# A whole-model kernel on one core: weight layouts packed into single transfers, a chunk fetched in quarters, PSUM copies put on one engine, and a third of the modulation sums placed elsewhere

## The reference, cut to what matters

```python
# adaptive modulation: six vectors of D per layer (shift, scale, gate for the mixer, then for the experts)
mod = silu(c) @ ada_w[l] + ada_b[l]                       # ada_w: (2, 1024, 6*1024)
h   = rms_norm(x, norm_mix[l]) * (1 + scale) + shift
def mix_gla_gdn(h, w_in, ...):                            # layer 0
    qa, ka, va, ga, za, qkvb, ab, bb, zb = _split(h @ w_in, AB_SPLITS)   # 512x1024 times 1024x3608
    gk = log_sigmoid(ga @ gla_w2 + gla_b) / 16
    oa = rms_norm(gla_chunked(qa, ka, va, gk)) * silu(za)
    qkvb = silu(causal_depthwise_conv(qkvb, conv_w))
    ob = rms_norm(gated_delta_chunked(...)) * silu(zb)
    return concatenate([oa, ob]) @ w_out
def moe(h, ...):  # every token takes 2 of 16 experts
    y = y + combine[:, e:e+1] * (silu(t @ w_gate[e]) * (t @ w_up[e]) @ w_down[e])
```

## Time and profile before

| | |
|---|---|
| median of 3 runs | 1425.98 us |
| time of the profiled execution | 1426.02 us |
| its span, first to last instruction | 1424.2 us |
| PE busy | 1232.5 us (87%) |
| DVE busy | 1066.1 us (75%) |
| ACT busy | 700.7 us (49%) |
| POOL busy | 327.7 us (23%) |
| mean granted clock of PE | 0.927 |
| moved by DMA | 337.68 MB |

### The profile page before, as it was taken

How to read it: one execution, slowest core, us unless ns; L and a number is a source line. 1 busy time by engine, 2 the same in 40 slices (tenths; PEclk the granted TensorE clock), 3 DMA queues, 4 the chain that set the end, 5 groups by cost and what they waited for, 6 DMA issues and landing times. The chain is left out here.

```text
span 1424.2 us, 16421 instructions
## 1 busy us (share of the span) xinstructions
PE 1232.5 (87%) x6452; PEld 931.3 (65%) x6452; DVE 1066.1 (75%) x1278; ACT 700.7 (49%) x918; POOL 327.7 (23%) x129
## 2 busy tenths in 40 slices
PE   2788996867999689999999859967995999999992
PEld 2567885657844668888888634434455788888881
DVE  6666885676845659989999657867266699999994
ACT  4222443232522247777777432248221577777770
POOL 0100000010000005466654200000001145566541
PEclk9899998989999589999999969979995999999996
DMA  9989435026031669999999092462016699999944
GB/s 363 284 292 315 133 119 192 15 94 263 2 123 46 261 211 376 383 381 369 380 373 378 25 366 76 135 233 105 16 64 231 242 368 380 370 385 388 379 176 193
DMA packets 60820, 337.68 MB, mean 237 GB/s; under 512 B 11885, under 2 KB 12638, under 8 KB 45636
## 3 DMA queue, kind: packets, MB, share of 16 engines
q1 hardware_dynamic: 48948, 313.11, 59.0%
q0 software_dynamic: 11360, 22.38, 4.5%
q10 hardware_dynamic: 432, 1.10, 0.2%
HBM read 325.08 MB, written 28.84 MB: 249 GB/s over the span
## 5 line engine op out<-in xcount | busy, mean ns | idle before, releaser
L1433 PE MATMUL ps<-ring_r,work_r 128*128 128x512 f32 x536 | 213.6, 399 | 0.0
L2476 DVE TENSOR_TENSOR ring_r<-ring,early_mod_r 128x2048 fp32r<-128x2048 f32 x76 | 182.4, 2429 | 25.7 <-ACT early_mod_r L1593 25.2
L1593 ACT ACTIVATE work<-ps 128x512 f32<-128x512 f32 (+3 forms) x125 | 84.3, 681 | 235.4 <-PE ps L1433 136.7
L849 POOL TENSOR_TENSOR work<-work,early_mod 128x1024 f32<-128x1024 f32 x30 | 162.5, 5416 | 147.2 <-ACT work L1593 147.2
L1431 PE MATMUL ps<-early_mod_r,work_r 128*128 128x512 f32 x468 | 188.9, 404 | 7.7 <-DVE work_r L2779 4.7
L1432 PE MATMUL ps<-early_mod_r,work_r 128*128 128x512 f32 x468 | 185.0, 395 | 0.0
L1593 ACT ACTIVATE work_r<-ring 128x2048 fp32r<-128x2048 f32 (+2 forms) x87 | 133.7, 1558 | 85.6 <-PE ps L954 85.4
L1593 ACT ACTIVATE early_mod_r<-ring 128x2048 fp32r<-128x2048 f32 x79 | 147.5, 1909 | 0.3 <-PE ps L1433 0.3
L1431 PE MATMUL ps<-work_r 128*128 128x512 f32 x324 | 132.6, 409 | 6.8 <-DVE work_r L2779 4.7
L2476 DVE TENSOR_TENSOR ring_r<-ring,work_r 128x2048 fp32r<-128x2048 f32 x52 | 130.7, 2538 | 4.5 <-ACT work_r L1593 4.5
L1432 PE MATMUL ps<-work_r 128*128 128x512 f32 x324 | 129.5, 400 | 0.0
(11 more groups left out here) (320 smaller groups left out, 2311.0 us busy)
## 6 DMA issues: line engine op xcount, KB each, us to landing
ring<-in_moe_w_up_dram SPq DMA_DIRECT2D x33, 2048.0 KB, 10.4
early_mod<-in_ada_w_dram SPq DMA_DIRECT2D x80, 512.0 KB, 4.5
ring<-in_moe_w_gate_dram SPq DMA_DIRECT2D x19, 2048.0 KB, 9.6
hT<-in_moe_w_down_dram SPq DMA_DIRECT2D x16, 2048.0 KB, 9.9
ring<-in_moe_w_down_dram SPq DMA_DIRECT2D x15, 2048.0 KB, 10.2
work<-in_moe_w_gate_dram SPq DMA_DIRECT2D x14, 2048.0 KB, 10.5
ring<-in_ab_w_in_dram SPq DMA_DIRECT2D x7, 2048.0 KB, 10.1
ring<-in_ada_w_dram SPq DMA_DIRECT2D x8, 1024.0 KB, 17.1
```

Of the source, the lines that this page charges most:

```text
L849: return nc.gpsimd.tensor_tensor(yb[buf], yb[buf], mod[:, 5 * D:6 * D], ALU.mult)
L1433: return mm(out, a_hi, w_lo, start=False, stop=last_)
L1593: return nc.scalar.activation(out, in_, fn, **kw)
L2476: v.tensor_tensor(half_of(l, m, half, True), half_of(l, m, half), highs[(2 * m + half) % MHIGHS].bitcast(F32), ALU.subtract).then_inc(SV.s ...
```

## The change

It has six parts.

1. The 24 columns of chunk 1 are packed on the host to one array of 128 rows by 192 values (`ab_small`) and fetched by one transfer; the 12 parameters in SBUF's `par` area come as one array `params` by one transfer, so that POOL issues 2 parameter loads in place of 13.
2. Chunks 4 to 7 are fetched in quarters of 512 KB: `load_ab_quarter(n + 3, q)` stands in step (n, q) of SP's queue for n = 1 to 4, ahead of that step's side loads. Before, the whole chunk n + 4 stood behind step n's side loads.
3. All copies out of PSUM in the projection are ACT's, but that of `small`, which is DVE's.
4. Odd chunks use banks 4 and 7 in place of 0 and 1 for tiles 0 and 1 (`job_bank`); PE waits for the last copy of the same bank (`last_in`).
5. 5 sides in place of 6 stand in the projection, and 3 in place of 2 in the mixers: `mix_sides` takes 8, 2, 4, 2 and four times 2 steps. In chunk 0 stand 2 steps in place of 8, in chunks 4 to 6 four each in place of 5, in chunk 7 six in place of 5, in chunks 2 and 3 ten each as before. In step q = 3 DVE takes its side steps between and behind its copies.
6. In the overflow block `split_low(j, 2, 1)` moves ahead of `hidden_`.

```diff
--- before.py
+++ after.py
@@ -384,7 +386,8 @@
 
         def loaded(c):
 
-            return 16 * (c // RING + 1)
+            last_ab = first[("abo", 0)] - 1
+            return 16 * (c // RING + 1 + (3 if c > last_ab - RING else 0))
 
         def slot(c):
             return ring[:, c % RING]
@@ -473,8 +476,8 @@
         smallT = carve("work", SEQ)
 
         SIDE = [(0, 2 + i) for i in range(4)] + [(1, i) for i in range(6)]
-        SIDE_A = 6
-        per_step = {0: (2, 2, 2, 2), 1: (0, 0, 0, 0), 2: (2, 3, 2, 3), 3: (2, 3, 2, 3), 4: (1, 1, 1, 2), 5: (1, 1, 1, 2), 6: (1, 1, 1, 2), 7: (2, 2, 1, 0)}
+        SIDE_A = 5
+        per_step = {0: (0, 0, 0, 2), 1: (0, 0, 0, 0), 2: (2, 3, 2, 3), 3: (2, 3, 2, 3), 4: (1, 1, 1, 1), 5: (1, 1, 1, 1), 6: (1, 1, 1, 1), 7: (3, 2, 1, 0)}
         side_at, _u = [], 0
         for n in range(8):
             for c in per_step[n]:
@@ -616,12 +619,17 @@
 
         split_chunks = [(first[("ab", 0)] + n, 24 if n == 1 else 512, 3 * 2048) for n in range(8)]
 
+        def small_weights(of, c):
+            return of[:, c % RING].rearrange("p k f -> p (k f)")[:, 0:KD * SMALL].rearrange("p (k f) -> p k f", k=KD)
+
         def quarter(i):
 
             c, w, at_ = split_chunks[i // 4]
             k = slice(2 * (i % 4), 2 * (i % 4) + 2)
             high = area_r["work"][:, at_ + D * (i % 3):at_ + D * (i % 3) + D].rearrange("p (k f) -> p k f", k=2)
-            return ring[:, c % RING, k, 0:w], high[:, :, 0:w], area_r["ring"][:, c % RING, k, 0:w]
+            if w == SMALL:
+                return small_weights(ring, c)[:, k], high[:, :, 0:w], small_weights(area_r["ring"], c)[:, k]
+            return ring[:, c % RING, k], high, area_r["ring"][:, c % RING, k]
 
         def quarter_used(i):
 
@@ -646,7 +654,7 @@
             if kind == "small" and t:
                 emptied.append(emptied[-1])
                 continue
-            e = "s" if kind in ("za", "zb") or j % 2 else "v"
+            e = "v" if kind == "small" else "s"
             emptied.append((e, counts[e]))
             counts[e] += 1
 
@@ -660,6 +668,10 @@
             emptied.append((e, counts[e]))
             counts[e] += 1
         NJ = len(jobs)
+
+        def job_bank(n, t):
+            return bank((4, 7, 2, 3)[t] if n % 2 else t)
+
 
         def emptier(j):
 
@@ -706,12 +718,13 @@
             def load_ab(n):
                 c = first[("ab", 0)] + n
                 if n == 1:
-                    free(c)
-                    sp.dma_start(slot(c)[:, :, 0:RANK], rows(a["ab_w_in"][0], slice(C_GA, C_GA + RANK))
-                                 ).then_inc(small_in, 16)
-                    load(c, slot(c)[:, :, RANK:RANK + 8], rows(a["ab_w_in"][0], slice(C_AB, C_AB + 8)))
+                    load(c, small_weights(ring, c), a["ab_small"].rearrange("p (k f) -> p k f", k=KD))
                 else:
                     load(c, slot(c), rows(a["ab_w_in"][0], slice(AB_COLS[n], AB_COLS[n] + 512)))
+
+            def load_ab_quarter(n, q):
+                c, k = first[("ab", 0)] + n, slice(2 * q, 2 * q + 2)
+                load(c, slot(c)[:, k], rows(a["ab_w_in"][0], slice(AB_COLS[n], AB_COLS[n] + 512))[:, k])
 
             def side_load(u):
                 i, k = u // KD, u % KD
@@ -745,11 +758,11 @@
                 side_load(u)
             for n in range(8):
                 for q in range(4):
+                    if 1 <= n < 5:
+                        load_ab_quarter(n + 3, q)
                     for u in side_at[4 * n + q]:
                         if u + 3 < KD * SIDE_A:
                             side_load(u + 3)
-                if n + 4 < 8:
-                    load_ab(n + 4)
             side_put(SIDE_A - 1)
             for u in range(KD * SIDE_A, KD * SIDE_A + 3):
                 side_load(u)
@@ -910,19 +923,8 @@
 
             nc.gpsimd.memset(side_pad, 0.0).then_inc(pad_ready, 1)
             pool.wait_ge(chunk_in[0], 32)
-            param(w2aug[0:SMALL + 1, :], a["gate_rows"])
-            param(conv_w.rearrange("p c k -> p (c k)"), a["conv_cols"])
-            param(gla_gain, bc(a["gla_norm"][0]))
-            param(gdn_gain, bc(a["gdn_norm"][0]))
-            param(q_gain, bc(a["swa_q_norm"][0]))
-            param(k_gain, bc(a["swa_k_norm"][0]))
-            param(sink, bc(a["swa_sinks"][0]))
-            param(router_w, a["router_w"].rearrange("(p k) e -> p k e", p=P))
-            param(router_b, bc(a["router_bias"]))
-            param(a_log, bc(a["gdn_a_log"][0]))
-            param(dt_bias, bc(a["gdn_dt_bias"][0]))
+            param(params, a["params"])
             param(pos_i[:], a["pos_cols"])
-            param(gain_col, a["gain_cols"])
             pool.wait_ge(phase_done, 3 * 2)
             for z_ in (xt, vn, st_b[:, 0], ku_b):
                 nc.gpsimd.memset(z_, 0.0).then_inc(init_pool, 1)
@@ -1012,22 +1015,24 @@
                         _, high, low = quarter(qi)
                         for t in ((0, ) if kind == "small" else range(TT)):
                             j = 4 * n + t
-                            if q == 0 and n:
-                                pe.wait_ge(*emptier(j - 4))
-                            if q == 0 and n == 2 and t:
-                                pe.wait_ge(*emptier(j - 8))
                             if n == 0 and t == 0:
                                 pe.wait_ge(norm_act.sem, norm_act.at(0, f"hi{2 * q + 1}"))
                                 pe.wait_ge(norm_dve.sem, norm_dve.at(0, f"lo{2 * q + 1}"))
+                            place = (n % 2, t) if t < 2 else t
+                            if q == 0:
+                                if place in last_in:
+                                    pe.wait_ge(*emptier(last_in[place]))
+                                last_in[place] = j
+                            out_ = job_bank(n, t)
                             for k in range(2):
                                 kk = 2 * q + k
                                 first_, last_ = kk == 0, kk == KD - 1
                                 if kind[0] == "f":
-                                    ins = parts_mm(bank(t), (high[:, k, cols(t)], low[:, k, cols(t)]), (hT_high[:, kk], hT_low[:, kk]), first_, last_)
+                                    ins = parts_mm(out_, (high[:, k, cols(t)], low[:, k, cols(t)]), (hT_high[:, kk], hT_low[:, kk]), first_, last_)
                                 elif kind == "small":
-                                    ins = parts_mm(bank(t)[0:SMALL], (high[:, k], low[:, k]), (hT_high[:, kk], hT_low[:, kk]), first_, last_)
+                                    ins = parts_mm(out_[0:SMALL], (high[:, k], low[:, k]), (hT_high[:, kk], hT_low[:, kk]), first_, last_)
                                 else:
-                                    ins = parts_mm(bank(t), (hT_high[:, kk, cols(t)], hT_low[:, kk, cols(t)]), (high[:, k], low[:, k]), first_, last_)
+                                    ins = parts_mm(out_, (hT_high[:, kk, cols(t)], hT_low[:, kk, cols(t)]), (high[:, k], low[:, k]), first_, last_)
                             if q == 3:
                                 ins.then_inc(proj_pe.sem, sum(proj_pe.one("job") for _ in range(TT if kind == "small" else 1)))
                         if n == 2 and q == 1:
@@ -2202,20 +2205,26 @@
                     for q in range(4):
                         if 4 * n + q + 2 < 32:
                             low_part(q0 + 4 * n + q + 2)
-                        for u in side_at[4 * n + q]:
-                            side(u)
-                        if q == 3:
+                        sides = iter(side_at[4 * n + q])
+                        if q < 3:
+                            for u in sides:
+                                side(u)
+                        else:
                             for t in range(TT):
                                 j, kind = 4 * n + t, AB_KIND[n]
                                 if emptied[j][0] == "v" and not (kind == "small" and t):
+                                    for u in itertools.islice(sides, 1):
+                                        side(u)
                                     dve.wait_ge(proj_pe.sem, proj_pe.at(j, "job"))
-                                    src = bank(t)
+                                    src = job_bank(n, t)
                                     dst = {"qk": pqk[:, t], "v": pv[:, t]}.get(kind)
                                     if kind == "small":
                                         dst, src = smallT[0:SMALL, :], src[0:SMALL]
                                     elif kind[0] == "f":
                                         dst = qkvT[:, j - 12, 3:3 + SEQ]
                                     v.tensor_copy(dst, src).then_inc(proj_dve.sem, proj_dve.one("ev"))
+                            for u in sides:
+                                side(u)
                         if n == 2 and q == 3:
                             dve.wait_ge(GATE_PE.sem, GATE_PE.at(0, "small"))
```

(18 more changed lines are left out.)

23 lines of the change are left out of this document (15 added, 8 removed).

## The result

The changed kernel takes 1413.08 us (median of 4 runs, 1408.20 to 1414.38), the kernel before 1427.09 us on the same chip (4 runs, 1425.82 to 1429.11). The ratio is 0.9894 with a 95% interval of 0.9866 to 0.9922: about 1.1% faster, and at the predicted 1413.0 us. The profiled execution took 1414.14 us, its span is 1412.2 us where that of before is 1424.2: 12.0 us less, 13.0 were forecast.

A forecast was written before the change was run, and what follows sets the result against it. PE was taken to bound the projection, interrupted by DVE's queue that the DMA engines feed late; in the mixers DVE's side steps stand in the chain. -21.2 + 8.9 - 0.7 = -13.0 us gave 1413.0 us, range 1409 to 1417.

The forecast's parts named there:

- Projection, -21.2 us: Projection: five PE holes released by DVE go (16.1 us), with half clock behind them (1.97, 1.37 and 1.7 us).
- rival A: Projection: DMA engines keep pacing chunks 2 and 3, fourth and fifth hole return as low-part waits; 1420.3 us, chance 0.16.
- Mixers, +8.9: Mixers: the eight side steps moved there add 8.9 us, from 5 to 13.
- (a): Gates: an eighth side step ahead of the gate product, its load landing late, adds 2.2 us.
- (b): Before the first GLA tile: a second side step adds 1.4 us.
- (c): Behind GLA: a fourth side step, whose load can only be issued late, adds 2.4 us.
- (d): Ahead of the inverses: one more side step adds 1.3 us.
- (e): Levels of the inverses: a second side step in each of four costs 0.56 us, partly hidden; 1.6 us in all.
- The pauses move along with the loads: Inverses: PE's two pauses, just behind the 4 MB weights' issue, move with that later issue rather than vanish; kept in the forecast.
- Rival B: Inverses: PE's pauses vanish because the 4 MB start later, 4.3 us less; 1408.7 us, chance 0.12.
- Overflow, -0.7: Overflow block: the moved split fills DVE's 2.65 us idle before the multiplication; the next split then waits only for ACT, -0.7 us.
- Rivals C and D: C: each added mixer step costs a load round trip, 1448.7 us, 0.05. D: ACT gates the projection, 1426.7 us, 0.07.

The follow-up runs named there:

- e2_sides: Kernel before with only the side steps moved (40 in the projection instead of 48, eight more in the mixers): 1426.63 us, ratio 0.9989.
- e1_copies: Kernel before with only the changed kernel's copies out of PSUM (ACT, but for `small`) and banks: 1411.82 us, ratio 0.9881.
- e4_back: Changed kernel with its eight moved side steps back in the projection, where DVE was idle: 1403.55 us, ratio 0.9822.
- e5_over: Changed kernel with the overflow block's old order, the multiplication ahead of the last split: 1415.15 us, ratio 0.9909.
- e7_late: Changed kernel with the eight steps back in the projection, spread earlier, and the output projection's weights issued only behind the last level: 1398.63 us, ratio 0.9792.
- e12_after_late: Changed kernel with the output projection's weights issued only behind the last level: 1408.54 us, ratio 0.9854.
- e9_thin_levels: Changed kernel with the second side step of each of four levels, and its load, cut to 8 of 1024 columns: 1407.30 us, one run.

## Why the prediction was right, and where its terms were off

- **Projection, -21.2 us: measured -20.8.** All five holes, both groups of 24 matmuls and the clock came as forecast; its end is at 209.08 us, 209.1 was forecast. The sides of chunks 2 and 3 ended at 118.0 us (119.7 forecast), so rival A's slack of 3.4 us was some 5.
- **Layouts, 0: neither shown nor refuted in the changed kernel.** The working put about 3 us into small pieces; by its own rows it is 3.9 (2.18 MB at 320 / 0.91 = 352 GB/s are 6.2 of 10.1 us). Alone the layouts bring the first side's start forward by 5.4 us (57.49 to 52.07 us) and are worth 3.16 us. But that comes from the first hole, which e2_sides closes without them, so 0 on top of the sides can be right. e1_copies, with neither, is left with a hole of 2.00 us to rival A; whether the six side loads fewer or the layouts take it away wasn't run apart.
- **Quarters, 0: measured 0**, within 1.3 us of slack. The rival by the Trainium skill's fixed cost of about 2 us for a transfer ("DMA: Bandwidth & Descriptors", Anatomy of one DMA), taken as serial, would have given a difference of 12 us of DMA time, and none is seen.
- **Mixers, +8.9: measured +12.1 in this execution.** The four programs with 24 full steps and the weights at their old place gave 8.5, 10.8, 12.1 and 15.1 us over the 114.2 of before; e4_back, with 16, gave 0.7. (a), (b), (c) as a wait and (d) hold to 0.2 us each: 7.5 us, 7.3 forecast. The step that failed is (e), 1.6 us for the second step in each level: the levels' idle time apart from the pauses is 0.88 us and was 0.86, so it cost nothing. What was left out is two terms: PE's own work at half clock, 4.0 us (1.0 in GLA, 1.3 in the levels, 1.7 at the opening of GDN), and pauses that grew by 0.7. That the sum was only 3.2 us too low is in part luck, since (e) stood in for some of them. The opening ran at half clock in two of the four, behind last pauses of 3.02 and 3.04 us; behind 1.44 (e2_sides) and 1.38 us it did not. e5_over, with all 24 steps, has it in 1.90 us:

```profile
293.98:329.91 35.93, 31.04 (x960) 30.13 (x960) 27.45 (x50) 10.66 (x29) 0.00 (x0) 0.95 0.60 206
329.91:331.81 1.90, 1.90 (x17) 1.90 (x18) 0.00 (x0) 1.83 (x5) 0.00 (x0) 1.00 1.05 382
```

- **"The pauses move along with the loads": right in size, not in place.** Their length goes with the loads, as e7_late, e12_after_late and e9_thin_levels show. Their places don't move: the first two stand at the same matmuls as before, shrunk from 4.87 to 2.51 us, and a third one of 3.02 us has come under the moved 4 MB. Rival B named the right thing, pauses that vanish when the loads come later; its condition, loads behind the levels, wasn't met by the change. The loads went out at 320.36 us with the levels running to 332 us.
- **Overflow, -0.7: measured 1.0 us by comparison of traces,** of which 0.65 is PE's wait, the mechanism that was forecast. The further 1.7 us of this pair of traces is the stretch of 3.4 us at half clock that four of the five traces of the old order have.
- **Rivals C and D:** the four added steps in the levels cost PE no wait, and the four ahead of them 1.3 to 2.4 us each, not 5.6; no wait of PE in the projection is released by ACT. What nobody forecast is that the moved steps didn't need the mixers: DVE had the idle time for all eight in the projection, 5.36 us in chunk 0 and the rest in chunks 5 to 7, and some 10 us were to be had that way.

The sum in this pair of traces: the start -0.4, projection -20.8, mixers +12.1, overflow -2.7, all the rest -0.2: -12.0 us. The forecast of -13.0 came out near it because the mixers' 3.2 us too little and the overflow's 2.0 us too little stand against each other: the main term, the projection, was right by its mechanism, and the closeness of the total is luck to that extent.

## What to carry to other kernels

A queue that serves two masters is read by what stands behind each wait: work moved out of the queue that interrupts PE pays even where its engine is not full, but look first for idle time of the same engine in the same stage before giving the work to a stage whose chain runs through it. Where two parts of a change cure the same hole, or one part's gain is waited for again at the next wait, what each gives alone says little of what it gives with the others, even if the sum happens to fit; ask of each what the hole becomes without the other. Before a longer stage is put down to the work that was added to it, split it into the engine's own work, its waits and its pauses: here the added steps stood in the levels and cost nothing in them. And a bulk load that nobody waits for still has a place to be: here 4 MB issued behind, not during, a dense stretch of small matmuls gave 4.8 us.

## What the runs showed of the hardware that was not expected

- **PE pauses for its own instruction stream when the DMA engines are busy.** Two stretches of the changed kernel that end with such a pause, at DMA shares of 0.66 and 0.92:

```profile
305.00:317.33 12.33, 9.82 (x330) 9.59 (x327) 10.23 (x18) 2.74 (x8) 0.00 (x0) 1.00 0.66 215
320.40:328.00 7.60, 4.58 (x159) 4.44 (x154) 6.41 (x11) 0.95 (x3) 0.00 (x0) 1.00 0.92 316
```

  The same work at a share of 0.07 to 0.14 has one pause of 0.78 us (e7_late). The DMA queues of kind "instruction" have a packet group at 315.0 and at 325.6 us, 2.3 and 2.4 us ahead of the ends of the pauses at 317.33 and 327.99 us. And the places are fixed in PE's stream: in all 14 traces every such pause stands, within two matmuls, at one of the same three places among the levels' 960, with 126 matmuls between the first and second place and 254 between the second and third (the x126 and x254 of the rows above), whatever the time and the loads. That these fetches are what PE waits for is inferred from places and times; that the loads make the pauses long is shown by the edits.
- **The granted clock differs between executions of the same instructions.** With the same 24 steps and the 4 MB at the same place the opening of GDN ran at 0.50 in two traces and at 1.00 in two, and the overflow block at the order of before had its stretch of 3.40 us at half clock in four of five. The Trainium skill ("TensorE: Matmul & The Clock Gate", HAM oscillation) has waits bring the clock down; the traces agree that it falls behind waits (10.41 us ahead of a stage at 0.63, a pause of 3.02 us ahead of 6.58 us at 0.50), but which matmuls it catches isn't the same from one execution to the next: behind the pauses of 2.08 and 2.79 us of before the levels stayed at 1.00, and in e4_back they have 3.4 us at half clock behind one of 2.46. Differences of 2 us in one stage of one pair of traces are no evidence without a second trace.
